# Moving four on-chip transfers per group from SyncE's queue to ACT's, in a two-layer float32 decoder trunk

## The reference

```
cond = silu(c)
for i in range(2):
    sh_m, sc_m, g_m, sh_f, sc_f, g_f = split(cond @ mod_w[i] + mod_b[i], 6)
    h = x * (1 + sc_m) + sh_m
    y = stick_breaking_attention(h)   if i == 0   else  short_conv_mixer(h)
    x = layer_norm(2**0.5 * x + (1 + g_m) * y)
    h = x * (1 + sc_f) + sh_f
    y = square(relu(h @ w1 + b1)) @ w2 + b2          # 2048 -> 8192 -> 2048
    x = layer_norm(2**0.5 * x + (1 + g_f) * y)

short_conv_mixer:  b, c, u = split(h @ w_in, 3)      # 2048 -> 3 x 2048
                   y = causal_conv_width3(c * u) + conv_b
                   return (b * y) @ w_out
```

## Time and profile before

| | |
|---|---|
| median of 3 runs | 2335.05 us (2332.59 to 2339.29) |
| the profiled execution | 2338.55 us, its span 2336.8 us |
| mean granted TensorE clock | 0.985 |
| busy: PE, weight load, DVE, ACT, POOL | 2230.2, 1862.1, 1729.9, 1128.6, 7.7 us |
| DMA, HBM read | 650.14 MB, mean 278 GB/s; 623.12 MB |
| chain that ended last | PE 69%, DVE 14%, DMA 6%, issue 5%, ACT 4%, SPq 2% |

### The profile page before, as it was taken

The page is one execution under the profiler, slowest core; times in us unless marked ns, Lnnn a source line. Parts: engine busy times, 40 slices in busy tenths (PEclk is TensorE's granted clock), DMA queues, the critical chain, the costliest instruction groups (busy, mean ns, idle before and its releaser), DMA issues.

```text
span 2336.8 us, 27641 instructions
## 1 busy us (share of the span) xinstructions
PE 2230.2 (95%) x10534; PEld 1862.1 (80%) x10534; DVE 1729.9 (74%) x1790; ACT 1128.6 (48%) x1409; POOL 7.7 (0%) x25
## 2 busy tenths in 40 slices
PE   6999999988999999999899999999899999999998
PEld 5999987866887787787787787888678888788876
DVE  7899989875777676777777799887665666655657
ACT  4777783644344435434445443345433553453542
POOL 0000000000000000000000000000000000000000
PEclk9999999999999999999999999999999999999999
DMA  9999999687888887888867998976677777766673
GB/s 354 387 386 398 397 326 338 213 299 275 311 278 285 285 297 264 293 296 260 289 200 285 330 313 314 323 262 233 226 261 229 247 249 239 237 205 196 199 245 106
DMA packets 306868, 650.14 MB, mean 278 GB/s; under 512 B 22049, under 2 KB 53297, under 8 KB 304689
## 3 DMA queue, kind: packets, MB, share of 16 engines
q1 hardware_dynamic: 303776, 631.33, 79.1%
q10 hardware_dynamic: 2960, 17.05, 1.8%
HBM read 623.12 MB, written 2.10 MB: 268 GB/s over the span
## 4 chain that ended last, share of the span: by engine, by line
PE 69%; DVE 14%; DMA 6%; issue 5%; ACT 4%; SPq 2%; ACTq 0%; DVEq 0%
PE bank L1325 20%; PE bank L1326 20%; PE bank L1327 20%; DVE w_low L961 5%; DMA stage<-stage 4%; DVE mod_acc L917 3%; PE bank L1315 2%; PE bank L1318 2%; PE bank L1317 2%; SPq L530 2%; ACT w_high L656 2%; ACT stage L832 1%; DVE stage L1154 1%; DMA mod_raw<-in_mod_w 1%; DVE hid_low L1161 1%
## 5 line engine op out<-in xcount | busy, mean ns | idle before, releaser
L961 DVE TENSOR_TENSOR w_low<-raw,w_high 128x1024 fp32r<-128x1024 f32 x752 | 909.1, 1220 | 532.5 <-ACT w_high L656 531.3
L656 ACT ACTIVATE w_high<-raw 128x1024 fp32r<-128x1024 f32 x752 | 781.3, 1056 | 912.5 <-PE bank L1327 891.8
L1325 PE MATMUL bank<-w_high,h_high 128*128 128x512 f32 x1632 | 647.8, 397 | 50.4 <-DVE w_low L961 50.3
L1326 PE MATMUL bank<-w_low,h_high 128*128 128x512 f32 x1632 | 642.7, 394 | 0.0
L1327 PE MATMUL bank<-w_high,h_low 128*128 128x512 f32 x1632 | 642.2, 393 | 0.0
L1325 PE MATMUL bank<-w_high,hid_high 128*128 128x512 f32 x1120 | 441.5, 394 | 24.0 <-DVE hid_low L1161 23.6
L917 DVE SCALAR_TENSOR_TENSOR mod_acc<-mod_raw,cond,mod_acc 128x1024 f32<-128x1024 f32 x345 | 441.7, 1280 | 20.7 <-DMA mod_raw<-in_mod_w 16.3
L1326 PE MATMUL bank<-w_low,hid_high 128*128 128x512 f32 x1120 | 439.7, 393 | 0.0
L1327 PE MATMUL bank<-w_high,hid_low 128*128 128x512 f32 x1120 | 439.7, 393 | 0.0
L1325 PEld LDWEIGHTS bank<-w_high,h_high 128*128 128x128 f32 x1632 | 310.8, 190 | 129.6 <-DVE w_low L961 58.2
L1327 PEld LDWEIGHTS bank<-w_high,h_low 128*128 128x128 f32 x1632 | 310.7, 190 | 65.8
(11 more groups left out here) (145 smaller groups left out, 1077.4 us busy)
## 6 DMA issues: line engine op xcount, KB each, us to landing
raw<-in_mlp_w SPq DMA_DIRECT2D x512, 512.0 KB, 4.9
mod_raw<-in_mod_w SPq DMA_DIRECT2D x368, 512.0 KB, 7.0
raw<-in_attn_w_qkv SPq DMA_DIRECT2D x96, 512.0 KB, 9.8
raw<-in_conv_w_in SPq DMA_DIRECT2D x96, 512.0 KB, 5.4
stage<-stage SPq DMA_DIRECT2D x176, 128.0 KB, 3.3
raw<-in_attn_w_o SPq DMA_DIRECT2D x32, 512.0 KB, 7.1
raw<-in_conv_w_out SPq DMA_DIRECT2D x32, 512.0 KB, 5.6
mod_raw<-in_mod_w SPq DMA_DIRECT2D x32, 256.0 KB, 6.4
```

The source lines that it names most:

```text
L656: act.activation(chunk_slots(n)[0], raw[:, n % NCH], ACT.Copy).then_inc(high_done, 1)
L961: dve.tensor_tensor(low_, raw[:, n % NCH], high.bitcast(F32), ALU.subtract).then_inc(raw_used, 1)
L1325: pe.matmul(dst, high[:, k, c], wh, start=first, stop=False, skip_group_check=True)
L1326: pe.matmul(dst, high[:, k, c], wl, start=False, stop=False, skip_group_check=True)
```

## The change

The four transfers, their waits and their semaphore stay as they are, and so do all other programs. `swap_quads` moves from SP's program into ACT's: `highs(w)` calls it first thing if the group before, w - 1, is one of the 44. In ACT's order it so stands behind the fourth high half of group w (made at the end of `highs(w - 1)`) and the wait for the end of group w - 1, and ahead of the fifth high half of group w.

```diff
@@ SP's program
-            def swap_quads(u):
-                i = u - U_CIN
-                if 0 < i <= NG:
-                    sp_.wait_ge(y_copied, i)
-                else:
-                    sp_.wait_ge(post_done, CREDIT_STAGE + (u if i <= 0 else u - NG))
-                sp_.wait_ge(banks_free, UNIT_GROUPS[u] + BANK0 + CREDIT_BANKS + 1)
-                for a in range(QUADS):
-                    sp_.dma_start(feat_quads[:, a, :], turned_quads[32 * a:32 * (a + 1)]).then_inc(swapped, 16)
-
-            swap_at = {(w + 1) * NCH + SLOTS - 1 + NCH: u for u, w in enumerate(UNIT_GROUPS)}
             for n in range(N_HEADS + 2 * AHEAD, N_CHUNKS):
                 load_chunk(n)
-                if n in swap_at:
-                    swap_quads(swap_at[n])
                 load_tiles(TILE_AT[n - AHEAD], TILE_AT[n - AHEAD + 1])
@@ ACT's program
+            def swap_quads(u):
+                i = u - U_CIN
+                if 0 < i <= NG:
+                    act.wait_ge(y_copied, i)
+                else:
+                    act.wait_ge(post_done, CREDIT_STAGE + (u if i <= 0 else u - NG))
+                act.wait_ge(banks_free, UNIT_GROUPS[u] + BANK0 + CREDIT_BANKS + 1)
+                for a in range(QUADS):
+                    act.dma_start(feat_quads[:, a, :], turned_quads[32 * a:32 * (a + 1)]).then_inc(swapped, 16)
+
             def highs(w, late=None, first=SLOTS):
 
+                if w - 1 in UNIT_GROUPS:
+                    swap_quads(UNIT_GROUPS.index(w - 1))
                 for j in range(first, NCH):
                     high(w * NCH + j)
                     if late and j == SLOTS + 1:
```

## The result

The changed kernel takes 2375.66 us (median of 4 runs, 2371.09 to 2378.18) against 2335.74 us for the kernel before, run beside it on the same chip: a ratio of 1.0168, interval 1.0147 to 1.019. It is slower, as forecast, but by 40 us and not by 10, and outside the range given. The profiled run took 2371.09 us with a span of 2369.4.

The account below looks back on a forecast made before the run. PE, busy 95% of the span, bounds the kernel, with 74.3 us of stalls for late low halves. Conv +15, residual +4, MLP +1 and landing -10 make +10 on the 2335.05 us median: 2345 us, range 2328 to 2362.

Parts of the forecast that it names:

- The hold: After each group's transposes: DVE waits 3.65 us for ACT's fifth high half, behind four issues taking 2.5 us in all.
- The conv groups: Eight groups computed on DVE, without idle time for the hold, +15 us; two with the residual beside them, +4 us.
- is more, not less: Eight DVE conv groups: cost exceeds +15 us if part of the 12.66 us idle is spent waiting for PE's chunks.
- The residual group: Conv groups with the residual beside them (2): PE's 1.36 us stall becomes 5.0 us; +4 us, 1 to 8.
- The landing: Transfers on ACT's queue no longer stand behind SP's loads and land sooner in backlogged groups: -10 us, ends 0 and -48.
- turn-taking between rows of 1, 2 and 4 KB: On the shared DMA engines: the four's rows alternate with the loads' longer rows, landing some 3 us sooner at 916.2.
- SP gets 2.5 us per group back, nothing follows: SP's queue: freed of the four issues it gains 2.5 us per group, with no effect on the time.
- second rival: Landing as before, since transfers share the engines with the backlog; only the 20 us of costs stay, 2355 us; chance 0.20.
- fourth rival: ACT issues slowly, over 1 us each, so DVE is held 5 us and more: 2370 us; chance 0.06.
- MLP groups' own cost, 1 us: The 32 MLP groups: DVE's later idle time holds the 3.65 us; 1 us on all of them, at most 6.

Follow-up runs that it names:

- e6: Kernel before, SP still issuing all transfers; ACT only waits for the transposes ahead of its fifth high half: 2337.37 us, ratio 1.0007.
- e9: Kernel before, but in the 12 conv groups ACT issues two of the four transfers and SP the other two: 2351.38 us, ratio 1.007.
- e1: Kernel before with only the 12 conv groups' transfers issued by ACT, the MLPs' by SP as before: 2363.87 us, ratio 1.0123.
- e3: Changed kernel, with SP held where it used to issue the four until the transposes are done: ratio 1.0181 to before.
- e5: Changed kernel with the four issues one place later in ACT's program, behind the fifth high half: ratio 1.046 to before.
- e4: Kernel before, with only the modulation tiles loaded ahead of the four transfers on SP's queue instead of behind: ratio 1.0071.
- e7: Changed kernel, with SP held until ACT has issued the four and made the fifth high half: ratio 1.0085 to before.
- e10: e8 with the MLPs' four transfers issued by ACT, SP waiting until they are out: 2299.13 us, ratio 0.9849 to before.
- e8: Kernel before with the four transfers one raw load earlier in SP's queue: 2305.28 us, ratio 0.9869.
- e14: e10 with SP held one raw load earlier still in the MLP: 2283.3 us, ratio 0.9783 to before.

## Why the prediction was wrong, point by point

**The hold was right.** ACT's four issues take 627 ns each in the median (forecast 0.6), DVE stands 3.8 to 5.0 us behind the transposes (median 3.9, forecast 3.65), ended by ACT's high half.

**The conv groups: mechanism right, term mis-sized.** Forecast 15 + 4 us, measured 25. The eight groups that DVE computes, after the change (one of them, and the sum), against the earlier trace rows:

```profile
1356.90:1385.90 29.00, 25.02 (x98) 19.87 (x97) 24.92 (x34) 8.17 (x9) 0.00 (x0) 0.88 0.83 297
...
sum 203.00, PE 184.11 PEld 147.64 DVE 169.12 ACT 66.43 POOL 0.00; mean PE 23.01 PEld 18.46 DVE 21.14 ACT 8.30 POOL 0.00
```

DVE's wait for the high halves in them (nine waits: the eight holds and one of 0.9 us):

```profile
DVE w_low L959 <- ACT w_high L641: 32.8, 9, 4.4
```

DVE is busy 169.12 us, about as before (170.24), and idle 33.9 where it was 12.66. The stretch grew by 20.1 us and not 15. Two terms of that sum missed by about 2.5 us each: the eight holds are 31.9 us and not 29.2, and 11.8 us of them were absorbed, not the 14.2 (12.66 of idle time and 1.5 at the end) that the prediction counted on. It had said of the idle time that the cost "is more, not less" if part of it is spent waiting, and did not price it. The same eight groups in e6, e9 and e1 show the curve: holds of 9.4, 23.8 and 31.9 us in all lengthen them by 2.1, 13.8 and 20.0, so that beyond the first 9.4 us about 0.8 us is lost for each us held. The residual group was forecast well. DVE and PE, against the earlier trace rows:

```profile
1292.44 1.31 DVE L1152 STREAM_TRANSPOSE stage<-bank 128x512 f32<-128x512 f32 x2
...
1297.66 2.36 DVE L959 TENSOR_TENSOR w_low<-raw,w_high 128x1024 fp32r<-128x1024 f32 x2 [3.91 <-ACT w_high L641]
```
```profile
1298.94 0.79 PE L1323 MATMUL bank<-w_high,h_high 128*128 128x512 f32 x1 [5.68 <-DVE w_low L959]
```

PE's stall of 1.36 us became 5.68 (forecast 5.0), and that group's loss went from 3.3 to 8.4 us (forecast about +4).

**The landing: the step that failed.** The term was -10, "in ACT's queue they do not" stand behind loads. Measured in the MLP is +7 in all, where -10 + 1 was forecast: 16 of the 23 us by which the forecast falls short of the span's 33. Three things showed in that step's place:

- In the group on which the term rested, the four did not get past what had been issued before: 9.88 against 9.82 us, and 9.28 to 10.12 against 8.61 to 9.82 over all profiles with T at that point. The turn-taking between rows of 1, 2 and 4 KB, from which the 3 us were worked out, didn't show as a gain there; whether it takes place, no run tells.
- Loads issued beside the four delay them: e3 is no better than the change, and e5, with a load among them in every MLP group, costs 107 us.
- SP, with its wait gone, issues a 512 KB load ahead. The prediction asked what the four had ahead of them on SP's queue and not what had been kept behind them. It noted "SP gets 2.5 us per group back, nothing follows"; e4 prices what follows, on one queue, at 17 us.

The rule of the Trainium skill ("DMA: Bandwidth & Descriptors", Issuing engines are not separate DMA queues), that transfers of all engines interleave on the same 16 engines and a second issuer only saves issue time, was given 0.20 as the second rival; this case's trace agrees with it, with 9.88 against 9.82. Of the rivals it was the nearest to what happened in the MLP. Even that rival, 2355 us, had the landing unchanged, and it got later. The fourth rival's number, 2370 us, lies nearest to the measured one, but its mechanism did not occur: ACT's issues took 627 ns and not over 1 us.

**MLP groups' own cost, 1 us: nothing speaks against it.** e6 has no cost there (96.8 against 103.2), and e7, which holds ACT as the change does but keeps the loads back, has an MLP loss 5 to 8 us below the kernels with the MLP of before. So DVE's idle time covers the hold of 4 us, as the earlier trace rows had it, or whatever is left of its cost is smaller than what e7 gains by keeping the loads back longer; the runs give only the difference. What remains of the forecast gain is those 5 to 8 us of e7, and it needs a wait in SP's program that the change doesn't have.

**Sum.** Conv +25, MLP +7 make 32 of the span's 33 us. The medians are 40 us apart because the profiled run of after lies 4.6 us below its median, and that of before 2.8 above.

**What stays open.** Whether the four on ACT's queue with all loads held back (e10) truly beat the same order on SP's (e8): the medians are 6 us apart (10 of MLP loss), but the intervals of the two ratios overlap. SP is held 1.2 us longer in e10, which may be all of it or a part; the runs don't divide it.

## What to carry to other kernels

When an issue moves to another engine's queue, price two things: the compute queued behind its wait and its issue time on the new engine (here four at 0.63 us plus the wait; once the next engine's idle time was used up, about 0.8 us of each us held went into the length), and what the old queue, freed of both, now issues ahead of it. In this kernel the order of issue worked as the priority of a transfer, across the two queues too: put the small transfers that a chain waits for ahead of bulk loads, and hold the loads until they are out (e14, -2.2%). Before counting on idle time to absorb a delay, add up both over the stretch: 12.66 us of idle time took 11.8 of the 31.9 us of holds here, and the rest went into the length.

## What the runs showed of the hardware

- A second queue gave no way past the largest backlog: last landing at 9.88 us from ACT's queue, 9.82 from SP's, in the same group with the same loads ahead.
- One 512 KB load issued about 0.9 us ahead of four transfers of 128 KB took their landing from 3.1 to 3.3 us to 4.4 to 5.0; over the kernel, with SP's order changed on one queue (e4) or two (the change), the median went from 3.3 to 3.9 us. L of this group came back within 0.25 us for either order, over seven profiles.
- With the loads kept back the four landed 2.5 to 4.0 us after their issue in the MLP groups of e14; the shortest landing is 2.5 us on either queue.
- In the eight conv groups after the change PE's granted clock was 0.88 and 0.94 in the two in which PE stood idle longest for a low half, 3.3 and 4.9 us, and 1.00 in the other six, whose idle stretches are at most 2.1 us; the mean over the 12 groups is 0.98 before and 0.97 after. So the price of a long stall has a part in which PE then runs at the lower of its two levels. Over the 12 groups it was busy 276.60 us where it had been 269.93, with the same instructions.
